# Routing chain of a two-layer trunk kernel: seven tiles' choice moved into the loop, one-hot rows written in three wide instructions, one projection moved up, gate weights issued behind the experts' weights

## What is computed

```python
h = h + y @ w_o[i]
m = rmsnorm(h, ffn_norm_g[i])
h = h + hier_moe(m, ...)                       # 4 groups x 8 experts, the two best of the best group
gate = jax.nn.sigmoid(rmsnorm(h, ple_norm_g[i]) @ ple_gate_w[i])
e = rmsnorm(p[i] @ ple_proj_w[i], ple_post_norm_g[i])
h = h + gate * e

def hier_moe(m, wg, bg, we, be, w_gate, w_up, w_down):
    g_idx = jnp.argmax(t @ wg + bg, axis=-1)               # group of each token
    ...                                                    # softmax and top 2 inside the group
    order = jnp.argsort(flat_e)                            # tokens sorted by expert
    ...
    def expert_block(args):                                # 128 tokens of one expert
        hb = jax.nn.silu(xb @ w_gate[e]) * (xb @ w_up[e])
        return (hb @ w_down[e]) * w_b[:, None]
```

## Time and profile before

| what | us |
|---|---|
| median of 3 runs (2132.74 to 2134.62) | 2133.2 |
| profiled execution, own time | 2132.33 |
| its span, first to last instruction | 2130.5 |
| TensorE busy | 1981.0 (93%) |
| VectorE busy | 1028.4 (48%) |
| ScalarE busy | 638.6 (30%) |
| GpSimd busy | 374.8 (18%) |
| mean granted clock of TensorE | 0.973 of full |

### The profile page before, as it was taken

How to read it: one execution, slowest core, us unless ns; L and a number is a source line. 1 busy time by engine, 2 the same in 40 slices (tenths; PEclk the granted TensorE clock), 3 DMA queues, 4 the chain that set the end, 5 groups by cost and what they waited for, 6 DMA issues and landing times.

```text
span 2130.5 us, 35243 instructions
## 1 busy us (share of the span) xinstructions
PE 1981.0 (93%) x8952; PEld 1107.7 (52%) x8952; DVE 1028.4 (48%) x2327; ACT 638.6 (30%) x1521; POOL 374.8 (18%) x542
## 2 busy tenths in 40 slices
PE   6999899999879999999979998999998799999898
PEld 3555576655445545544435555776554455445443
DVE  2489778654432111235424897786544321112353
ACT  3333366522111111132133433665221111111311
POOL 2332100021012222210022321000210222221100
PEclk9999999999879999999989999999998899999999
DMA  7011241000499999965210112410013999999522
GB/s 256 15 30 30 67 152 46 11 30 29 169 331 391 382 380 379 390 229 204 85 29 15 30 30 74 145 46 11 30 49 140 356 395 374 374 378 348 179 89 98
DMA packets 122224, 362.00 MB, mean 170 GB/s; under 512 B 18853, under 2 KB 54005, under 8 KB 105220
## 3 DMA queue, kind: packets, MB, share of 16 engines
q1 hardware_dynamic: 105028, 318.74, 41.3%
q0 software_dynamic: 14784, 33.59, 4.3%
q10 hardware_dynamic: 2304, 8.39, 1.0%
HBM read 319.50 MB, written 59.51 MB: 178 GB/s over the span
## 4 chain that ended last, share of the span: by engine, by line
PE 80%; DMA 12%; DVE 3%; issue 2%; ACT 2%; SPq 1%; POOL 0%; ACTq 0%; POOLq 0%; DVEq 0%
PE ps L1845 32%; DMA region_c<-in_moe_w_up_dram 8%; PE ps L2231 7%; PE ps L2019 6%; PE ps L1866 4%; PE ps L2227 4%; PE ps L2252 4%; PE ps L2064 4%; PE ps L2043 3%; PE ps L1814 3%; PE ps L1940 2%; PE ps L2246 2%; PE ps L2153 2%; PE ps L2212 2%; DMA region_a<-in_moe_w_up_dram 2%
## 5 line engine op out<-in xcount | busy, mean ns | idle before, releaser
L1845 PE MATMUL ps<-region_b,region_c 128*128 128x512 f32 x1024 | 449.7, 595 | 3.3 <-DVE region_c L1300 2.8
L1845 PEld LDWEIGHTS ps<-region_b,region_c 128*128 128x128 f32 x1024 | 192.5, 191 | 228.3 <-issue 227.8
L1845 PE MATMUL ps<-region_a,region_c 128*128 128x512 f32 x512 | 224.3, 592 | 0.0
L1725 DVE SCALAR_TENSOR_TENSOR region_a<-region_a,ps 128x128 f32<-128x128 f32 x66 | 23.4, 354 | 385.2 <-ACT region_a L1163 385.2
L2231 PE MATMUL ps<-region_c,region_a 128*128 128x512 f32 x336 | 148.8, 596 | 14.5 <-DMA region_c<-in_moe_w_up_dram 14.5
L2019 PE MATMUL ps<-region_c 96*128 96x512 f32 (+3 forms) x384 | 152.4, 507 | 5.4 <-ACT region_a L1095 4.0
L1845 PEld LDWEIGHTS ps<-region_a,region_c 128*128 128x128 f32 x512 | 96.5, 190 | 116.6 <-issue 116.6
L1163 ACT ACTIVATE region_a<-ps 128x128 f32<-128x128 f32 x66 | 21.8, 330 | 362.8 <-PE ps L2231 243.3
L2231 PEld LDWEIGHTS ps<-region_c,region_a 128*128 128x128 f32 x336 | 62.2, 190 | 94.4 <-issue 94.4
L1501 DVE TENSOR_REDUCE neg_max<-ps 128x1 f32<-128x128 f32 (+7 forms) x128 | 96.8, 756 | 17.5 <-PE ps L2026 14.6
L958 ACT COPY region_c<-ps 128x512 f32<-128x512 f32 x48 | 28.0, 584 | 246.7 <-PE ps L1814 175.7
(11 more groups left out here) (360 smaller groups left out, 3189.1 us busy)
## 6 DMA issues: line engine op xcount, KB each, us to landing
region_c<-in_moe_w_gate_dram SPq DMA_DIRECT2D x44, 1024.0 KB, 10.4
region_c<-in_moe_w_up_dram SPq DMA_DIRECT2D x44, 1024.0 KB, 17.3
region_c<-in_moe_w_down_dram SPq DMA_DIRECT2D x44, 1024.0 KB, 13.0
region_a<-in_moe_w_gate_dram SPq DMA_DIRECT2D x22, 1024.0 KB
region_a<-in_moe_w_up_dram SPq DMA_DIRECT2D x22, 1024.0 KB
region_a<-in_moe_w_down_dram SPq DMA_DIRECT2D x22, 1024.0 KB
region_c<-choice_outputs SPq DMA_DIRECT2D x32, 512.0 KB, 4.5
qk_heads<-gains SPq DMA_DIRECT2D x32, 384.0 KB, 3.9
```

The lines of the kernel that those rows point to most:

```text
L1845: ins = mm(dst, lhsT[:, k, :], w[:, k, a:b], start=(k == 0), stop=(k == KD - 1))
```

## The change

Four things are changed, in both layers.

**Choice of seven tiles.** TensorE computes tile 6's router product between the two halves of the high W_o product of tile 7 (`g_early`, `w_hi`). VectorE works out the group and the first expert of tiles 0 to 6 (`first_of_most`, 11 instructions) ahead of the residual add of tile 7's high half, the second expert (`second_of_most`, 5) ahead of tile 7's norm, and the one-hot sums (`hots_of_most`, 2) behind tile 7's transposes. Only tile 7 is left for the chain (15 instructions of at most 128x32). The softmax sums, which stood in the chain, go to its end. Counts and ranks of seven tiles are multiplied ahead of tile 7's.

**Shorter links.** Counts arrive divided by 128, blocks are rounded by adding and subtracting a large constant, a sum that three VectorE instructions made comes from TensorE, several instructions no longer wait for the one before, and two are moved behind the list of blocks.

**Wide one-hot rows.** Three instructions over all 16 rows take the place of the 32.

**Projection and gate weights.** The transposes of p stand in tile 7's step ahead of tile 6's transposes, projection 0 ahead of tile 7's transposes (in banks 4 and 5), projection 1 behind the last router product. The gate weights and gains are issued behind the loop over the experts' weights.

```diff
-    sp.wait_ge(*W_pe.before(TILES * l + TILES))
-    sp.dma_start(ple_g, I["ple_gate_w"][l].rearrange("(k p) n -> p k n", p=P)).then_inc(ple_loaded, 16)
...
     block_loop(sp, n, weights)
+    for k, src in ((BRANCH, I["ple_post_norm_g"]), (FFN, I["ple_norm_g"])):
+        sp.dma_start(gains[:, k], src[l].partition_broadcast(P)).then_inc(post_loaded, 16)
+    sp.dma_start(ple_g, I["ple_gate_w"][l].rearrange("(k p) n -> p k n", p=P)).then_inc(ple_loaded, 16)
+    guarded(sp, l < DEPTH - 1, lambda: load_mix((l + 1).with_bounds(max_val=DEPTH - 1)))
...
-        b, dst = (2 + 2 * u, e_out[u]) if t < EARLY_P else (6 - 2 * u, e_late[u])
+        b, dst = (4 - 2 * u, e_out[u]) if t < EARLY_P else (6 - 2 * u, e_late[u])
...
+    def first_embedded(t, u, i):
+        if isinstance(t, int) and t == TILES - 1:
+            act.wait_ge(*FX.square.before(24 * l + 2 * TILES))
+            embedded(0)
+
+    lag_loop(act, [(-1, norm_m), (2, later(norm(1))), (1, later(turn(1))), (0, p_turned, 1), (-1, first_embedded), (-1, turn_m), (3, late(c_tanh)), (3, late(c_yT_evac))])
...
+    def first_of_most():
...
+        link(v.tensor_reduce(sm(0)[:, 0:MOST], gl_[:, 0:MOST], AX.X, ALU.max), "g_max_most")
+        link(v.tensor_tensor(below, gl_[:, 0:MOST], bc(sm(0)[:, 0:MOST], NG), ALU.is_lt), "g_lt_most")
...
+        seek_most(e_in, sm(4), sm(5), 1)
+        hot_most(sm(5), hot1, 1)
...
+    def second_of_most():
+        link(v.scalar_tensor_tensor(rest[:, 0:MOST], hot1[:, 0:MOST], -2 * BIG, e_in[:, 0:MOST], ALU.mult, ALU.add), "rest_most")
+        seek_most(rest, sm(6), sm(7), 2)
+
+    def hots_of_most():
+        hot_most(sm(7), hot2, 2)
+        link(v.tensor_tensor(picked_b[:, 0:MOST], hot1[:, 0:MOST], hot2[:, 0:MOST], ALU.add), "picked_most")
+
+    def first(t, u, i):
+        def go():
+            g_main(TILES - 2, 0, PAIRS - 1)
+            first_of_most()
+        guarded(v, i > PAIRS - 2, go)
...
+    lag_loop(v, [(-1, second_choice), (-1, norm_m), (2, later(norm(1))), (1, later(turn(1))), (3, late(conv_centre)), (-1, turn_m),
+                 (-1, hot_choice), (0, w_main(0)), (3, late(conv_scale)), (3, late(conv_silu)), (0, first, 1), (0, w_main(1)),
+                 (-1, g_others), (3, late(conv_out))])
...
+    link(v.tensor_reduce(sm(0)[:, LAST], last(gl_), AX.X, ALU.max), "g_max_last")
+    link(v.scalar_tensor_tensor(last(gs(3, TILES)), last(gl_), sm(0)[:, LAST], iota64[:, 0:NG], ALU.is_lt, ALU.add), "g_cand_last")
...
+    link(v.tensor_tensor(last(picked_b), last(hot1), last(hot2), ALU.add), "picked_last")
...
+    v.wait_ge(*K_pe.after(l, "counts"))
+    v.tensor_scalar(nb_f[:, 0:1], ps[0:NE, 6, 0:1], (HALF - 1 - (P - 1) / 2) / P, ROUND, ALU.add, ALU.add)
+    link(v.tensor_scalar(nb_f[:, 1:2], ps[0:NE, 6, 0:1], (P - 1) / 2 / P, ROUND, ALU.add, ALU.add), "cnt_nb")
...
-    link(v.tensor_tensor(both, n_full, n_half, ALU.add), "both")
-    link(v.tensor_scalar(quarter, both, 0.5, 0.25, ALU.mult, ALU.add), "quarter")
-    link(v.tensor_scalar(whole, quarter, ROUND, None, ALU.add), "whole")
...
+    link(v.tensor_scalar(whole, bank(6, 196, 197), 0.25, ROUND, ALU.add, ALU.add), "whole")
...
-    for c in range(2 * TILES):
-        t, k = divmod(c, 2)
-        v.tensor_scalar(hot_s[:, c, :], iota[:, :], fields[:, 0, t, k:k + 1], None, ALU.is_equal)
-        ins = v.tensor_scalar(hot_b[:, c, :], iota[:, 0:POS], blk_f[:, t, k:k + 1], token[:, t, k:k + 1],
-                              ALU.is_equal, ALU.mult)
-    ins.then_inc(*K_vec.next("hots"))
...
+    v.tensor_tensor(hot_b, count_up(POS), each(blk_f, POS), ALU.is_equal).then_inc(*K_vec.next("in_block"))
+    v.tensor_tensor(hot_s, count_up(P), each(fields[:, 0], P), ALU.is_equal).then_inc(*K_vec.next("in_slot"))
+    v.wait_ge(*K_vec.after(l, "in_block"))
+    v.tensor_tensor(hot_b, hot_b, each(token, POS), ALU.mult).then_inc(*K_vec.next("hots"))
...
+    def first_project(t, u, i):
+        if t < TILES - 1:
+            return
+        pe.wait_ge(proj_loaded, 16 * l + 16)
+        pe.wait_ge(*G_vec.before(end - 1))
+        pe.wait_ge(*W_vec.before(end))
+        settle(pe, passed)
+        project(0)
...
+    def g_late(t, u, i):
+        if t == TILES - 1:
+            pe.wait_ge(*P_act.after(TILES * l))
...
+    static_loop([(0, w_lo), (1, later(turn(1))), (3, late(conv_back)), (0, turn_p), (-1, first_project), (-1, turn_m), (0, w_hi(0)),
+                 (-1, g_early), (0, w_hi(1)), (3, late(conv_turn)), (-1, g_late), (3, late(pointwise))])
...
+    project(1)
...
+    pe.wait_ge(*K_vec.after(l, "picked_most"))
...
+    for t in range(TILES - 1):
+        counted(t)
+    for t in range(TILES - 1):
+        ranked(t)
+    pe.wait_ge(*K_vec.after(l, "picked_last"))
...
+    counted(TILES - 1).then_inc(*K_pe.next("counts"))
+    ranked(TILES - 1).then_inc(*K_pe.next("ranks"))
```

More of the change, by code:

```diff
@@ new lines, in hot_most @@
+                def hot_most(where, hot, n):
+                    link(v.tensor_tensor(hot[:, 0:MOST], row(NE), bc(where[:, 0:MOST], NE), ALU.is_equal), f"hot{n}_most")
+                def first_of_most():
+                    v.wait_ge(*G_vec.before(TILES * l + TILES - 1))
+                    settle(v, passed)
+                    below, ahead, other = (gs(k, TILES)[:, 0:MOST] for k in (2, 3, 4))
+                    link(v.tensor_reduce(sm(0)[:, 0:MOST], gl_[:, 0:MOST], AX.X, ALU.max), "g_max_most")
+                    link(v.tensor_tensor(below, gl_[:, 0:MOST], bc(sm(0)[:, 0:MOST], NG), ALU.is_lt), "g_lt_most")
+                    link(v.tensor_tensor(ahead, below, row(NG), ALU.add), "g_cand_most")
+                    link(v.tensor_reduce(sm(3)[:, 0:MOST], ahead, AX.X, ALU.min), "g_first_most")
+                    link(v.tensor_tensor(other, row(NG), bc(sm(3)[:, 0:MOST], NG), ALU.not_equal), "g_ne_most")
+                    link(v.scalar_tensor_tensor(e_in[:, 0:MOST].rearrange("p t (g e) -> p t g e", g=NG),
+                                                other.unsqueeze(3).to_broadcast([P, MOST, NG, EPG]), -BIG,
+                                                el[:, 0:MOST].rearrange("p t (g e) -> p t g e", g=NG), ALU.mult, ALU.add), "e_in_most")
+                    seek_most(e_in, sm(4), sm(5), 1)
+                    hot_most(sm(5), hot1, 1)
+                    settle(v, passed)
@@ new lines, in largest_of_last @@
+                def largest_of_last(src, top, where, hot, n):
+                    link(v.tensor_reduce(top[:, LAST], last(src), AX.X, ALU.max), f"m{n}_last")
+                    link(v.scalar_tensor_tensor(last(cand), last(src), top[:, LAST], iota64[:, :], ALU.is_lt, ALU.add), f"cand{n}_last")
+                    link(v.tensor_reduce(where[:, LAST], last(cand), AX.X, ALU.min), f"i{n}_last")
+                    link(v.tensor_scalar(last(hot), iota64[:, :], where[:, LAST], None, ALU.is_equal), f"hot{n}_last")
```

225 lines of the change are left out of this document (120 added, 105 removed).

## The result

The changed kernel takes **2120.25 us** (2117.53 to 2120.75, four runs) where the kernel before takes 2132.97 in the same comparison: a ratio of **0.994 [0.9928, 0.9951]**, 12.7 us less. The profiled execution is the fastest of the four: 2117.53 us, a span of 2115.7, 14.8 less than the profiled one of before.

What follows compares the result with a forecast made beforehand. Transfers were taken to bound the experts' blocks, whose end follows the first weights' issue: 7.5 earlier less 0.5 for gate weights, 7.0 a layer, 14.0 in two, from 2132.3 to 2118.3, so 2119; range 2112 to 2129.

Steps and rivals of the forecast that it cites:

- The add: Last tile's residual add on VectorE: comes 3.0 us later, bounds 2.6 and 4.
- Add to logits: From the last residual add to the last tile's logits: logits 1.5 us later, bounds 1.5 and 3.4, full clock taken.
- rival 1: Clock falls anyway around the last router product, which takes 3.60 (plus 1.9); layer gains 3.4, time 2126; chance 0.20.
- Choice and counts: From last logits to counts on VectorE: counts go on 5.3 us earlier, with projection 1 as the new bound.
- The list of blocks: From counts to the first weights' issue: 2.2 us shorter, so the weights are issued 7.5 earlier.
- The token lists: One-hot rows on VectorE: three wide instructions take 4.7 us, minus 2.0; first block starts about 8 earlier.
- rival 2: Wide one-hot rows are slow, 9.4 us instead of 4.7: layer gains say 5, time 2124; chance 0.04.
- loss of 2.7: One-hot rows priced by elements alone, after a documentation rule: a loss of 2.7 where the profile rows give a 2.0 gain.
- The end of the blocks: End of the experts' blocks moves by as much as the first weights' issue, in each layer; weights 7.5 us earlier.
- The gate weights: Gate weights issued behind the last block's weights: nearly hidden, a cost of 0.5 us a layer, bounds 0 and 2.
- Rival 3: Start of the weights' stream moves but its end does not, refills setting it: 2131 to 2133; chance 0.08.
- Rival 4: Late gate weights hold up the fetch of the results by 8.5 or 10 us a layer: 2138; chance 0.05.

Runs made afterwards that it cites:

- e5: The changed kernel with short idle TensorE products filling its three pauses around tile 7's transposes: 2113.68 us, ratio 0.9907 to the kernel before.
- e3: The changed kernel with the thirty-two narrow one-hot instructions back in place of the three wide ones: 2127.62 us, ratio 0.9983 to the kernel before.
- e11: The kernel of e5 with gate weights, gains and mixer gain issued at their old, early place: 2119.86 us, ratio 0.9942 to the kernel before.
- e4: The changed kernel with gate weights, gains and mixer gain issued at their old place, ahead of the first experts' weights: 2120.10 us, ratio 0.9944.
- e1: The changed kernel with projection 1 moved from in front of the counts to stand with projections 2 and 3: 2118.51 us, ratio 0.9939.
- e8: The changed kernel itself run once more, unaltered, against another set of runs of the kernel before: 2120.82 us, ratio 0.9945.

## Why the prediction was right, and where by luck

The forecast was 2119, measured 2120.25. The mechanism held but for the clock, and the number is nearer than the steps are: 14.0 were forecast for two layers, 11.4 came, by two errors of opposite sign that are told below, and the medians moved by 12.7. The steps:

**The add.** 3.0 later forecast; 2.4 on the span's clock and 3.3 against the loop, and the 0.33 idle behind L1587 shows VectorE as the one that set it. Right.

**Add to logits.** 1.5 later forecast, 1.55 measured, but by luck, two things that cancel: ScalarE's squares and copy came as I put them, the loop stood 0.9 earlier by chance, and the router product took 2.65, neither the 1.87 I took nor rival 1's 3.60.

**Choice and counts: the step that failed.** "I take the full clock", and "5.3 earlier" from it. Measured 2.3 on the span's clock, and 1.4 and 3.1 in the two layers against the loop. The choice itself was right: 3.7 us from the logits to the picked row, 3.5 forecast. TensorE was the later one as I wrote, and by 3 us instead of 0.6, since projection 1 took 6.39 where I had 3.4 (3.68 at a clock of 1.00, in e5). Rival 1 was thus half true (its 1.9 for the router product is 1.73 by its own rows); its reason against itself (that the drop before stood behind an idle stretch twice as long as the longest pause left) did not hold: three pauses of 1.8, 0.7 and 1.1 us with work between them were enough. With the pauses filled (e5) the step is right: add to counts 14.2, where I had said 14.

**The list of blocks.** 2.2 less forecast; 5.27 instead of 7.72 between counts and weights, 2.45 less. Right.

**The token lists.** 1.2 + 2.3 + 1.2 forecast; 1.23, 2.28 and 1.22 measured, so rival 2 falls. The narrow form's fixed cost is confirmed by e3, where the thirty-two rows again take 6.7 on the clock. (The "loss of 2.7" for a cost by elements alone was the bound 9.4 less 6.7; 3072 elements at half of 1.2 us for 1024 make 1.8, so that loss would be 2.9.) Two numbers of this step were wrong to the good. I had the first block follow the weights 0.5 closer, 1.6 less up to 1 for the gather; it was 2.6: the token list is done 2.0 closer, and the wait behind it shrank by 0.6 instead of growing. And e3 shows this part worth some 8 us of the time, where the sum had nothing for it beyond the weights' 7.5.

**The end of the blocks.** That "the end of the blocks moves by as much as 588.48 does" was too simple, and this is the second error, of the other sign. The last weights moved 0.8 and 2.2 more than the first ones, since the pause behind the first three blocks shrank with the first block's earlier start. That made up for part of what the counts lacked: 7.0 a layer forecast, 3.8 and 7.7 measured at the fetch. That the two errors came out near each other is luck: with the clock at 1.00, as I assumed, my 2119 would have been 5 too slow (e5: 2113.7).

**The gate weights.** 0.5 a layer forecast, bounds 0 and 2. From the last weights to the fetch it takes 28.20 instead of 27.30 in the first layer, and 26.90 against 26.86 in the second: 0.9 and 0. The reason given, "this is why they must go", held for weights at 581 (e11) and made no difference for weights at 583.8 (e4).

**Rival 3** (end not moved) falls with the last weights' 4.7 and 7.7. **Rival 4** (slower by the gate weights) had a price of 0.9 in one layer instead of 8.5: the load landed at 930.1, 20.1 us behind its issue and 2.8 ahead of the fetch, with a DMA share of 0.81 and 0.49 in 924 to 932 where it was 0.00 and 0.01 before, while the last stores ran.

## What to carry to other kernels

When a chain is shortened, work out what TensorE does in the pauses that are left, and price the products behind them at both clock levels; here three short pauses close together brought the lower clock as the one long pause before had done, and a few idle products in them gave back 7 to 8 us. Where a stream of transfers starts with a fixed number of buffers, its end follows the later of two things, the first issue and the first block that frees a buffer, so look at both before shortening one (e1 moved the issue earlier and the third block later, and gained nothing that shows). Undo each part of a change alone: what the parts are worth singly need not add up to the whole (25 for 12.7 here), and one of several may be worth nothing yet.

## What the runs showed of the hardware

Three pauses of 1.77, 0.71 and 1.09 us, with 3.7 and 1.1 us of work between them, brought the granted clock from 1.00 to 0.50 in both layers of all six profiled executions that had them, but not at the same place: the router product behind them took 2.65 and 2.42 us in the change, 2.39 and 2.00 in e8, 1.98 and 1.97 in e4, 3.02 and 2.17 in e3, and projection 1 the rest of the loss (5.38 in e4's first layer). An estimate from one execution of what the lower clock costs is therefore off by 1 to 2 us at such a place.

Why the second layer's tail takes one of two lengths can be followed a step further in the traces. ScalarE's copy of the tail's third projection waits until the first one is stored, and the gate product stands behind a copy that ScalarE makes after it. ScalarE's third copy in the change (17.76) and in e5 (19.55), then the gate product in e5:

```profile
1989.30 1.01 ACT L1136 COPY region_c<-ps 128x1024 f32<-128x1024 f32 x1 [1.58 <-DMA projected<-region_c]
1988.44 1.01 ACT L1136 COPY region_c<-ps 128x1024 f32<-128x1024 f32 x1 [3.66 <-DMA projected<-region_c]
1991.23 7.13 PE L1903 MATMUL ps<-region_b,region_c 128*128 128x512 f32 x16 [0.91 <-ACT region_c L960]
```

In the five short tails that store is issued 7.8 to 8.1 us behind the fetch, and the third copy starts 5.7 to 6.6 behind its issue; in the nine long ones it is issued at 8.5 to 9.4, and the copy starts 7.5 to 8.3 behind it. The first three projections take 11.2 to 11.5 us in the short tails and 11.9 to 12.7 in the long ones. That a store issued half a us later ends two or more later is read from these fourteen executions; why it does was not tried.
